# Ten slots in place of five in the raw-weight ring while the experts' weights stream through

## The reference, cut to what matters

```python
def swiglu(x, wg, wu, wd):
    return (jax.nn.silu(x @ wg) * (x @ wu)) @ wd

def moe(x, router, wg, wu, wd):
    logits = (x @ router).astype(jnp.float32)
    top_logit, top_idx = lax.top_k(logits, TOP_K)        # 2 of 8
    top_w = jax.nn.softmax(top_logit, axis=-1)
    gates = jnp.sum(jax.nn.one_hot(top_idx, N_EXPERTS, dtype=jnp.float32) * top_w[..., None], axis=-2)
    y = jnp.zeros_like(x)
    for e in range(N_EXPERTS):
        y = y + gates[..., e:e + 1].astype(x.dtype) * swiglu(x, wg[e], wu[e], wd[e])
    return y
```

## Time and profile before

| | |
|---|---|
| median of 3 runs | 2304.9 us (2299.38 to 2305.33) |
| the profiled execution: its span | 2297.9 us, 7.0 us under that median; it has no time of its own beside the span |
| PE busy | 2219.4 us (97%) |
| DVE busy, ACT busy | 1569.8 us (68%), 1393.0 us (61%) |
| read from HBM | 394.48 MB, 172 GB/s over the span |
| the experts' stage | 1098 us to 1545 us of the span, 280 pieces |
| DMA in that stage | 309 GB/s, mean busy share of the 16 DMA engines 0.88 |

### The profile page before, as it was taken

How to read it: one execution, slowest core, us unless ns; L and a number is a source line. 1 busy time by engine, 2 the same in 40 slices (tenths; PEclk the granted TensorE clock), 3 DMA queues, 4 the chain that set the end, 5 groups by cost and what they waited for, 6 DMA issues and landing times.

```text
span 2297.9 us, 38597 instructions
## 1 busy us (share of the span) xinstructions
PE 2219.4 (97%) x16098; PEld 2067.3 (90%) x16098; DVE 1569.8 (68%) x2245; ACT 1393.0 (61%) x1918; POOL 21.7 (1%) x14
## 2 busy tenths in 40 slices
PE   8999999999999999998999999989989999998999
PEld 7999999999999999997877778779979999888999
DVE  6777556656477775564788888886867664785764
ACT  6875546544467755464777777776775554775553
POOL 0000000000000000000000000000000000000000
PEclk9999999999999999998999999999999999999999
DMA  7441234556554413251798888984414655423553
GB/s 260 153 140 59 96 108 158 175 170 184 165 174 151 148 56 102 93 170 62 272 313 303 312 302 318 319 300 137 144 55 150 190 182 167 153 82 101 193 184 129
DMA packets 112213, 398.12 MB, mean 173 GB/s; under 512 B 12576, under 2 KB 12704, under 8 KB 112032
## 3 DMA queue, kind: packets, MB, share of 16 engines
q1 hardware_dynamic: 112032, 395.58, 51.9%
HBM read 394.48 MB, written 1.05 MB: 172 GB/s over the span
## 4 chain that ended last, share of the span: by engine, by line
PE 77%; DVE 9%; DMA 7%; ACT 5%; issue 1%; DVEq 0%; SPq 0%; ACTq 0%
PE ps L411 76%; DMA raw<-stream 7%; DVE wlo L2020 5%; ACT whi L1260 2%; DVE h L2020 1%; ACT arena_r L1270 1%; DVE scr L2028 1%; ACT arena L1270 1%; DVE arena L2020 1%; ACT scr L1270 0%; DVE arena_r L2020 0%; ACT uh L1270 0%; ACT rst L1270 0%; DVE arena_r L2028 0%; PE ps L863 0%
## 5 line engine op out<-in xcount | busy, mean ns | idle before, releaser
L2020 DVE TENSOR_TENSOR wlo<-raw,whi 128x1024 fp32r<-128x1024 f32 (+2 forms) x762 | 905.1, 1201 | 439.2 <-ACT whi L1260 431.8
L1260 ACT ACTIVATE whi<-raw 128x1024 fp32r<-128x1024 f32 (+2 forms) x762 | 785.3, 1038 | 499.8 <-PE ps L411 418.8
L411 PE MATMUL ps<-uh,whi 128*128 128x256 f32 x2240 | 649.4, 290 | 3.3 <-issue 1.4
L411 PE MATMUL ps<-ul,whi 128*128 128x256 f32 x2240 | 633.4, 283 | 0.0
L411 PE MATMUL ps<-uh,wlo 128*128 128x256 f32 x2240 | 633.3, 283 | 0.0
L411 PE MATMUL ps<-arena_r,whi 128*128 128x256 f32 x2720 | 490.4, 283 | 7.1 <-DVE arena_r L2020 6.2
L411 PEld LDWEIGHTS ps<-uh,whi 128*128 128x128 f32 x2240 | 427.6, 191 | 14.0 <-issue 9.8
L411 PEld LDWEIGHTS ps<-ul,whi 128*128 128x128 f32 x2240 | 427.7, 191 | 6.7 <-issue 6.2
L411 PEld LDWEIGHTS ps<-arena_r,whi 128*128 128x128 f32 x2720 | 420.9, 190 | 11.3 <-issue 7.7
L411 PEld LDWEIGHTS ps<-uh,wlo 128*128 128x128 f32 x2240 | 427.5, 191 | 0.0
L411 PE MATMUL ps<-arena_r,wlo 128*128 128x256 f32 x1360 | 382.0, 281 | 0.0
(11 more groups left out here) (164 smaller groups left out, 1949.6 us busy)
## 6 DMA issues: line engine op xcount, KB each, us to landing
raw<-stream SPq DMA_DIRECT2D x694, 512.0 KB, 4.0
raw<-stream SPq DMA_DIRECT2D x64, 384.0 KB, 4.1
CO<-const SPq DMA_DIRECT2D x2, 704.5 KB, 7.7
h<-xT SPq DMA_DIRECT2D x4, 256.0 KB, 5.6
raw<-stream SPq DMA_DIRECT2D x4, 256.0 KB, 3.9
out<-h SPq DMA_DIRECT2D x4, 256.0 KB, 2.2
CO<-const SPq DMA_DIRECT2D x1, 704.0 KB, 7.5
arena<-pT SPq DMA_DIRECT2D x2, 256.0 KB, 3.2
```

Source lines behind the costliest of these rows:

```text
L411: return self.e.matmul(o, l, r, start=start, stop=stop, skip_group_check=True)
L1260: self.e.activation(M.whi[:, b:b + n], M.raw[:, a:a + n], ACT.Copy).then_inc(K.sem("weight_hi"), 1)
L2020: return self.e.tensor_tensor(o, a, b, op)
```

## The change

The ring has ten slots instead of five while the experts' pieces are issued (`NRAW + MORE`). The five new ones are two blocks of 1024 columns in `CO`, on the tables `ret`, `rotr`, `rcos` and `rsin`, which the change moves to the end of `CO` so that they stand together, and three blocks in the arena at 11264. `raw_slots` fixes for every piece its slot, how many times that slot has been used, and the piece that stood there before: it takes the slot whose last piece is oldest, among five for pieces before `marks["branch"] + AHEAD` and after the last expert piece, among ten between. The amount of work, the order of all instructions on PE, ACT and DVE, the sizes of the DMAs, `AHEAD` and `NSPLIT` stay.

```diff
+MORE = 5
...
-    for name, n in (("ident", 128), ("ones", 256), ("lvl", 2 * 7 * 32), ("causal", 384), ("ret", 4 * 384),
+    for name, n in (("ident", 128), ("ones", 256), ("lvl", 2 * 7 * 32), ("causal", 384),
                     ("negm", 128), ("half", 2), ("halves", 256), ("bones", 128),
-                    ("rotr", 128), ("rcos", 256), ("rsin", 256), ("rota", 128), ("acos", 256), ("asin", 256),
-                    ("jlt", 64)):
+                    ("rota", 128), ("acos", 256), ("asin", 256), ("jlt", 64),
+                    ("ret", 4 * 384), ("rotr", 128), ("rcos", 256), ("rsin", 256)):
...
+        self.raw = self.raw_slots(pieces, old.marks["branch"] + AHEAD) if old else []
+
+    @staticmethod
+    def raw_slots(pieces, first):
+        experts = [i for i, x in enumerate(pieces) if x[0].startswith("exp_")]
+        newest, turns, out = [-1] * (NRAW + MORE), [0] * (NRAW + MORE), []
+        for i in range(len(pieces)):
+            n = NRAW + MORE if first <= i <= experts[-1] else NRAW
+            j = min(range(n), key=lambda x: newest[x])
+            turns[j] += 1
+            out.append((j, turns[j], newest[j]))
+            newest[j] = i
+        return out
...
+        at = const_layout()[0]["ret"][0]
+        self.raw = [raw[:, i * CH:(i + 1) * CH] for i in range(NRAW)]
+        self.raw += [self.CO[:, at + i * CH:at + (i + 1) * CH] for i in range(2)]
+        self.raw += [AR[:, 11264 + i * CH:11264 + (i + 1) * CH] for i in range(3)]
...
-            if i >= NRAW:
-                if i - NRAW in K.split_no:
-                    self.wait_ge(K.sem("weight_lo"), K.split_no[i - NRAW] + 1)
-                else:
-                    self.wait_ge(*K.when("used", i - NRAW))
-            a = i % NRAW * CH
+            j, _, last = K.raw[i]
+            if last in K.split_no:
+                self.wait_ge(K.sem("weight_lo"), K.split_no[last] + 1)
+            elif last >= 0:
+                self.wait_ge(*K.when("used", last))
             src = M.stream[K.offset[i]:K.offset[i] + n * P].rearrange("(p n) -> p n", p=P)
-            self.e.dma_start(M.raw[:, a:a + n], src).then_inc(K.sem(f"raw{i % NRAW}"), 16)
+            self.e.dma_start(M.raw[j][:, 0:n], src).then_inc(K.sem(f"raw{j}"), 16)
```

More of the change, by code:

```diff
@@ L210, in landed @@
     def landed(self, i):
-        return self.sem(f"raw{i % NRAW}"), 16 * (i // NRAW + 1)
+        if self.old is None:
+            return None, 0
+        j, turn, _ = self.raw[i]
+        return self.sem(f"raw{j}"), 16 * turn
 class Ring:
@@ L253, in __init__ @@
         self.SM, self.CO = sb("SM", small_layout()[1]), sb("CO", const_layout()[1])
-        self.raw = sb("raw", NRAW * CH)
+        raw = sb("raw", NRAW * CH)
         self.whi, self.wlo = sb("whi", NSPLIT * CH, F32R), sb("wlo", NSPLIT * CH, F32R)
@@ L429, in piece @@
             self.wait_ge(*self.K.landed(i))
-            at = i % NRAW * CH
-            return i, v3(self.M.raw[:, at:at + n], ncol)
+            return i, v3(self.M.raw[self.K.raw[i][0] if self.K.raw else 0][:, 0:n], ncol)
         self.wait_ge(self.K.sem("weight_lo"), self.split + 1)
@@ L1258, in rounded @@
                 self.wait_ge(*K.when("used", K.split_at[j - NSPLIT]))
-            a, b = i % NRAW * CH, j % NSPLIT * CH
-            self.e.activation(M.whi[:, b:b + n], M.raw[:, a:a + n], ACT.Copy).then_inc(K.sem("weight_hi"), 1)
+            a, b = K.raw[i][0], j % NSPLIT * CH
+            self.e.activation(M.whi[:, b:b + n], M.raw[a][:, 0:n], ACT.Copy).then_inc(K.sem("weight_hi"), 1)
     def ln_exp(self):
@@ L2013, in rounded @@
             j, self.split = self.split, self.split + 1
-            a, b = i % NRAW * CH, j % NSPLIT * CH
+            a, b = K.raw[i][0], j % NSPLIT * CH
             self.wait_ge(K.sem("weight_hi"), j + 1)
-            self.tt(M.wlo[:, b:b + n], M.raw[:, a:a + n], M.whi[:, b:b + n].bitcast(F32), SUB).then_inc(
+            self.tt(M.wlo[:, b:b + n], M.raw[a][:, 0:n], M.whi[:, b:b + n].bitcast(F32), SUB).then_inc(
                 K.sem("weight_lo"), 1)
```

## The result

| | before | ten slots |
|---|---|---|
| median of 4 runs each, same chip | 2303.15 us (2299.38 to 2305.33) | 2267.57 us (2266.57 to 2268.75) |
| ratio, 95% interval | | 0.9854 (0.9836 to 0.9873) |
| span of the profiled execution | 2297.9 us | 2266.9 us |
| the experts' stage on PE | 445.5 us | 412.8 us |

The direction and the mechanism were right; the gain, 35.6 us between medians and 31.0 between the two spans, was larger than the 27 forecast.

What follows compares the result with a forecast made beforehand. The prediction took the experts' stage to be bound by a five-slot ring too short for its round trip. Waits of 29.2 us less 2 gave 27 off the 2297.9 span, 2271, plus 7 to the median: 2278 us, range 2271 to 2295.

Steps and rivals of the forecast that it cites:

- What bounds the stage: Experts' stage: five slots' round trip gives at best one piece per 1.49 us, PE uses one in 1.36 to 1.40.
- The rate of the DMA: Experts' stage with ten slots: 137.58 MB take 330 us at 417 GB/s, or 418 at 329, against PE's 416.
- My expectation that landing takes longer: Experts' stage: time from issue to landing should rise above 5.2 us, with more in flight, without harm.
- The head start: After the flag: SP can issue ten pieces instead of five, most landed by PE's first expert product; no separate gain priced.
- Rival B: Experts' stage: the stream gets 309 GB/s and no more, whatever the depth; gain 8.5 us, 2296 us; chance 0.08.
- The length of the stage without waits: Experts' stage on PE: priced at 416.3 us against 445.5, so 29.2 us is waiting, the most to gain.
- The end: Experts' stage, last product to last scatter: 3.7 us after deducting that product, waiting for ACT and DVE; no slot helps.
- DVE's bursts: After scatters and at experts' ends: DVE's low parts may come late; 2 us of waits left for them.
- Rival A: Experts' stage: casts and low parts stay late by themselves, leaving half the waits; gain 14 us, 2291 us; chance 0.19.
- From the span to the median: Whole kernel: the median of 2304.9 us lay 7 above the profiled span of 2297.9; these 7 were added to 2271.
- C: Experts' stage: the change does not bite, PE's waits follow from something else; within 0.3%, 2302 us; chance 0.05.
- D: Experts' stage: instruction fetches stand behind the DMA backlog, 6.3 us more per exposed fetch, up to 2379 us; chance 0.05.

Runs made afterwards that it cites:

- the kernel before once more: The kernel before the change, run again with no edit for a second trace and its variation; 2302.44 us median of 11, ratio 1.0004 to the kernel before.

## Why the prediction was right or wrong

The mechanism held; two sizes in the sum did not, and with them the lower end of the range. The first is the stage's length without waits, put at 416.3 us: the 29.2 us left over were called "the most that the change can give", and the stage became 32.8 us shorter. The second is the 7 us carried over from the span to the median: 0.7 us was measured. One reading of the earlier trace rows was off too, without weight: slice 20 moved 272 GB/s, not 300 or more.

**What bounds the stage: right.** The round trip of (5.2 + 1.06 + 1.2) / 5 = 1.49 us a piece against PE's 1.36 to 1.40 is borne out by the ends: five slots, even with a lead, 446 us; six, 415; seven and more, 413. The two waits of PE for one late landing went together. The pitch gives the threshold and not the size of the loss: 280 x 1.49 us are 417 us, hardly more than the 413 of the stage without waits. A turn of the ring in fact took 5 x 446 / 280 = 7.96 us on average, 0.5 more than the 7.46 counted. One part of that stands in the waits of the kernel before, 1098 to 1545 us, in the row between those of the earlier trace rows:

```profile
ACT whi L1260 <- PE ps L411: 34.2, 70, 1.8
```

So 70 casts were held by PE and not by a landing; while they were, a piece that may have landed kept its slot. How the rest divides was not measured.

**The rate of the DMA: right.** I took the upper end, 417 GB/s, by depth; 404 was shown in the stage itself. The lower end, 329 GB/s at a share of 0.98, was a reading of a shallow queue, not a limit: the changed stage runs at 332 with a share of 0.92. The limit of about 358 GB/s for loads, which the prediction weighed from the Trainium skill (DMA: Bandwidth & Descriptors, section Bandwidth), is there each core's part when both cores of a memory domain stream. This kernel runs on one core, and 404 GB/s was measured. Another page of the Trainium skill (Perfetto Trace Analysis, section Identifying Performance Opportunities) calls the occupancy of the 16 engines misleading and asks to go by the bandwidth instead; here 0.88 of share went with 309 / 404 = 0.76 of the rate.

**My expectation that landing takes longer: hardly.** It rose from 5.2 to 5.6 us. By 332 GB/s and 5.6 us, 1.86 MB are in flight, fewer than four pieces; by this estimate the other slots hold pieces that have landed and wait. Depth was needed less in flight than in stock.

**The head start: without weight in the sum.** Alone it gives nothing, against the 4 to 7.5 us that I expected of it before that run. The forecast gave it no price. Rival B's 8.5 us are a head start too (137.58 MB at 309 GB/s are 445 us, the stage as it was), but under a capped rate, and no run had one.

**The length of the stage without waits: the first term that failed, 5.5 us too long.** I had 416.3 us plus 2 for bursts of DVE; it is 412.8.
- Scatters and gathers were priced at the shortest gather of before, 2.28 us, as if nothing waited in it. Without late ACT work a scatter takes 1.91 and a gather 2.00 us, 4.3 us less over the thirteen.
- The end, 3.9 us from the last product to the last scatter, is 2.8 now: ACT, no longer behind with its casts, takes up the last result 0.4 us after that product's start and not 1.2. I had said that no slot helps it, and that the 3.5 us of waiting in it must stay; they are 2.4.
- The 2 us of DVE's bursts did not come: 0.3 us of waits for a low part are left. PE did not wait at the experts' ends, where I had counted a slim 0.4 us. Rival A is out.
- Against these, the products and transposes take 1.7 us more than I counted (368.4 us for the products with 0.3 of wait, against 366.6).

**From the span to the median: the second term that failed, 6.3 us.** This is the larger part. I carried over the 7 us that lay between the first profile's span and the median. In the traces taken since, an execution's time is 1.8 us above its span (2268.75 and 2266.9 with ten slots, 2302.44 and 2300.6 for the kernel before once more). So the first profile was one of the fast executions, at about 2299.7 with a median of 2303.15, while the profiled one of the changed kernel was the slowest of its four. The median of the changed kernel lies 0.7 above that span. What I took for an offset was mostly the spread between executions, and I should have carried it as a few us of uncertainty on either side of the range instead of 7 us on one side (eleven runs of the kernel before once more lie from 7.1 us below their median to 1.7 above it). The 35.6 us between medians hold some of this luck; the spans of the two profiled executions differ by 31.0.

Together: 5.5 for the stage, less 1.8 by which the rest of the profiled execution was longer, plus 6.3, is 10.0 of the 10.4 us between 2278 and 2267.6; the remainder is rounding in the forecast. The range was cut at the whole 29 us of waits, but part of the waiting was hidden in the numbers that I had taken as free of it, so that 29 was not the most.

**Rivals C and D.** C is out with the stage. D, instructions fetched behind the backlog, did not show: PE's loss to "issue" in the stage is 3.5 us in 14 times with ten slots, as before, and 9.5 in 22 times in the kernel with a load beside each piece, which is also 180 us longer.

## What to carry to other kernels

A ring whose slots come back only after landing and two more engines has a pitch of at least (round trip) / (slots). Compare that with the consumer's pitch in its runs of products, not with its average over the stage (413 / 280 = 1.47 us, which hides the difference), before looking at the share of busy DMA engines: here 1.49 against 1.36 to 1.40 us, and one slot more was worth 31 of 33 us, the four after it 2. And price the floor of a stage on stretches that wait for nothing at all; a section with no wait printed before it can still hold a neighbour's lateness.

## What the runs showed of the hardware

The DMA sustained about 404 GB/s of loads for one core beside busy PE, DVE and ACT, over 360 us, with pieces of 512 and 384 KB and extra loads of 224 KB. That is near the 417 GB/s of the kernel's start.

The executions of one kernel differ by several microseconds (2295.4 to 2304.1 for eleven of the kernel before once more) while the stage repeats within 1 us. A part of it is PE's clock. The kernel before once more reached its stage at 1102.62, the kernel with six slots, whose program is the same up to there but for the place of tables, at 1095.78. Most of these 6.8 us arise long before. Ahead of the router's pauses both have an unbroken run of 254 matmuls in the chain of waits, and it begins 5.6 us apart (start, us):

```profile
1033.39 36.08 PE ps L411 x254
...
1027.84 34.26 PE ps L432 x254
```

Matching the two traces matmul by matmul, 0.6 us of the distance stand from the first 70 us on. Most of the rest comes in three stretches in which the granted clock of the first was below 1.00 and that of the second was not. The first of the three, in the kernel before once more and then with six slots:

```profile
480.00:500.00 20.00, 16.89 (x131) 16.71 (x130) 9.63 (x14) 9.58 (x15) 0.00 (x0) 0.91 0.45 152
...
480.00:500.00 20.00, 16.89 (x143) 16.71 (x141) 11.08 (x15) 10.03 (x15) 0.00 (x0) 1.00 0.48 165
```

PE waited the same 3.11 us in both and was busy for the same 16.89 us, but at a mean clock of 0.91 it got through 131 matmuls and at 1.00 through 143 (some 5 of the 12 are the 0.6 us by which the same work lies apart). The other two, 615 to 635 and 730 to 750 us, show 0.91 against 1.00 as well. After the three the distance is 2.0, 4.0 and 5.6 us. The last 1.3 us come in and behind the run of 254, where the clock of both falls to 1.2 GHz (0.50 from 1060 to 1067 us in both traces). In the kernel before once more it was at 0.99 from 1040 to 1060 us, with PE busy all 20.00 us, so there it fell without a pause of PE. Why the clock falls in one execution and not in the other stays open.

In the kernel with a load beside each piece the granted clock is 0.97 over the stage, where it is 1.00 in all the others. There PE's weight loads waited 134.9 us for a low part and 41.2 for the silu. With five slots it is 1.00, so the clock has no part in the 33 us of this change.
